# An encoder layer on one core: the query, key and value weights in rows of two heads, half of heads 2 and 3 multiplied early

## What is computed

```
mod = silu(c) @ ada_w + ada_b                  # 2048 x 12288: shift1, scale1, gate1, shift2, scale2, gate2
h   = rms_norm(x) * norm1_g * (1 + scale1) + shift1
q, k, v = split(h @ w_in, 3)                   # w_in 2048 x 6144, 8 heads, 256 columns per head and part
for each head: two softmaxes of q k^T * 128^-0.5 - slope * |distance|, a = p0 - lambda * p1, o = a @ v
x1  = x + gate1 * (rms_norm(o) @ w_out)        # w_out 2048 x 2048
router: top group, top 2 of its 8 experts; SwiGLU experts, 32 of 2048 -> 2 x 512 -> 2048
out = rms_norm(x1 + gate2 * experts) * final_g
```

## Time and profile before

| | us |
|---|---|
| median of 3 runs | 1552.8 (1551.68 to 1553.72) |
| the profiled execution, its own time | 1552.36 |
| its span in the trace | 1550.6 |
| busy: PE, DVE, ACT, POOL | 1166.8, 630.0, 185.2, 118.0 |
| TensorE's mean granted clock | 0.883 of full speed |
| moved by DMA | 577.87 MB, mean 373 GB/s |

### The profile page before, as it was taken

One profiled execution on the slowest core, in us unless ns is written; L12 is line 12 of the kernel. 1 busy time (PEld: TensorE's weight loads), 2 busy tenths in 40 slices (PEclk: granted clock), 3 DMA queues, 4 the chain that ended last, 5 costly groups with the idle time before them and its releaser, 6 DMA issues.

```text
span 1550.6 us, 21165 instructions
## 1 busy us (share of the span) xinstructions
PE 1166.8 (75%) x8538; PEld 760.2 (49%) x8538; DVE 630.0 (41%) x1128; ACT 185.2 (12%) x391; POOL 118.0 (8%) x146
## 2 busy tenths in 40 slices
PE   2298899999999998876657657657657657756655
PEld 2187688888888887433324224224213223323322
DVE  6576775755886112354214213213213213213214
ACT  3000322222224211130000000000000000000002
POOL 4232111101211000000000000000000000000001
PEclk9599899999999999997978878888888878878978
DMA  9997999989998754799999999999999999999996
GB/s 312 348 349 267 340 371 368 356 299 354 319 373 289 278 198 176 303 429 373 429 427 427 430 427 428 430 427 428 430 427 428 430 427 429 428 427 430 425 427 242
DMA packets 128520, 577.87 MB, mean 373 GB/s; under 512 B 10474, under 2 KB 76096, under 8 KB 102996
## 3 DMA queue, kind: packets, MB, share of 16 engines
q1 hardware_dynamic: 101572, 474.37, 76.1%
q0 software_dynamic: 26896, 102.77, 18.4%
HBM read 575.02 MB, written 2.10 MB: 372 GB/s over the span
## 4 chain that ended last, share of the span: by engine, by line
PE 51%; DMA 37%; DVE 7%; another core or an unknown queue 2%; issue 1%; ACT 1%; SPq 0%; DVEq 0%; ACTq 0%
DMA ring<-in_moe_w_gu_dram 19%; DMA ring<-in_moe_w_d_dram 13%; PE psum L589 11%; PE psum L897 7%; PE psum L680 5%; PE psum L599 5%; PE psum L808 5%; PE psum L926 5%; DMA ring<-in_da_w_in_dram 4%; PE psum L949 3%; DVE arena L1216 2%; PE psum L630 2%; PE psum L672 2%; PE psum L570 1%
## 5 line engine op out<-in xcount | busy, mean ns | idle before, releaser
L897 PE MATMUL psum<-ring,ada_ring 128*32 128x256 f32 x3712 | 274.8, 446 | 141.2 <-DMA ring<-in_moe_w_gu_dram 141.2
L1216 DVE SCALAR_TENSOR_TENSOR arena<-ada_ring,silu_c,arena 128x512 f32<-128x512 f32 x360 | 270.6, 752 | 26.8 <-DMA ada_ring<-in_ada_w_dram 15.3
L897 PEld LDWEIGHTS psum<-ring,ada_ring 128*32 128x32 f32 x3712 | 124.0, 121 | 288.5 <-DMA ring<-in_moe_w_gu_dram 188.6
L926 PE MATMUL psum<-ring,arena 128*32 128x512 f32 x960 | 155.4, 792 | 30.3 <-ACT arena L1136 16.2
L589 PE MATMUL psum<-region_b,ring 128*128 128x256 f32 x768 | 169.5, 382 | 0.0
L589 PEld LDWEIGHTS psum<-region_b,ring 128*128 128x128 f32 x768 | 146.5, 192 | 19.4
L1559 DVE TENSOR_TENSOR arena<-psum,arena 32x512 f32<-32x512 f32 x108 | 74.2, 687 | 188.1 <-PE psum L926 176.6
L1542 DVE TENSOR_SCALAR arena<-arena 128x128 f32<-128x128 f32 x32 | 7.3, 227 | 347.9 <-ACT arena L1130 347.9
L456 POOL DMA_DIRECT2D ada_ring<-in_ada_w_dram x128 | 97.5, 764 | 371.1 <-DVE arena L1216 363.7
L1130 ACT ACTIVATE arena<-psum 128x128 f32<-128x128 f32 x32 | 8.9, 277 | 782.5 <-PE psum L897 737.9
L926 PEld LDWEIGHTS psum<-ring,arena 128*32 128x32 f32 x960 | 35.9, 132 | 126.0 <-issue 81.8
(11 more groups left out here) (229 smaller groups left out, 893.6 us busy)
## 6 DMA issues: line engine op xcount, KB each, us to landing
ring<-in_moe_w_gu_dram SPq DMA_DIRECT2D x124, 2048.0 KB, 25.6
ring<-in_moe_w_d_dram SPq DMA_DIRECT2D x62, 2048.0 KB, 24.7
ada_ring<-in_ada_w_dram POOLq DMA_DIRECT2D x64, 1024.0 KB, 9.9
ring<-in_da_w_in_dram SPq DMA_DIRECT2D x24, 2048.0 KB, 27.7
ada_ring<-in_ada_w_dram POOLq DMA_DIRECT2D x64, 512.0 KB, 9.7
ring<-in_da_w_out_dram SPq DMA_DIRECT2D x8, 2048.0 KB, 25.8
ring<-in_moe_w_d_dram SPq DMA_DIRECT2D x8, 512.0 KB, 18.7
region_a<-in_x_dram SPq DMA_DIRECT2D x1, 2048.0 KB, 13.6
```

The lines of the kernel that those rows point to most:

```text
L897: last = mm(psum[32 * n:32 * n + 32, B_GU, 0:256].rearrange("p (a b) -> p a b", a=2), x_items[:, k, SLOTS * i:SLOTS * (i + 1)], w[:, :, n ...
L926: last = mm(psum[32 * n:32 * n + 32, B_D + i % 2, :], hid_t[:, k, :], w[:, kk, n, :], start=k == 0, stop=k == FT - 1)
L1216: ins = v.scalar_tensor_tensor(out=acc[:, par, :], in0=w, scalar=silu_c[:, k:k + 1], in1=acc[:, par, :], op0=ALU.mult, op1=ALU.add)
```

## The change

1. **Rows of two heads.** W_in is loaded for two heads at a time, 512 columns (2 KB) per row. Heads 0 and 1, and the first half of heads 2 and 3: by quarters of the features (4 tiles, 1 MiB for each of q, k, v), two quarters of heads 0 and 1 in slots 0 to 2, two of heads 2 and 3 in slots 3 to 5. The second half of heads 2 and 3, and heads 4 to 7: by halves of the features (8 tiles, 2 MiB). A wide slot of heads 4 to 7 is released by the odd head of the pair, two slots with each product.
2. **Blocks of adaLN.** Blocks 0 and 1 stay. Blocks 2 to 7 are now 512 columns of scale1 (even) and of shift1 (odd), in rows of 2 KB, so `h_t` becomes ready in steps of 2, 2, 4, 4 and 4 tiles (`STEPS`).
3. **Half of heads 2 and 3 early.** Twelve pieces `pair_part(q, u)` of 8 matmuls (tiles 4q to 4q + 3) go among the early ones. ACT keeps each in SBUF (`keep_part`, 12 x 128x512), DVE adds the two quarters (3 x 128x1024). Later `rest_product` multiplies tiles 8 to 15 (16 matmuls), and DVE adds the kept half while it copies the product (`keep_rest`).
4. **The chunks.** Beside heads 2 and 3 DVE has 5 chunks each, beside heads 4 to 6 12 each and beside head 7 9, and PE has three sums in each of heads 4 to 7. The loops over heads are written out. `transpose_out(2)` moves into the first product of head 4.

The core of the diff (the semaphore counts follow from it):

```diff
+        STEPS = ((0, 2), (2, 4), (4, 8), (8, 12), (12, 16))
...
-            for n, (h, j) in enumerate(EARLY):
-                sp.wait_ge(ada_used, ADA_CH * EARLY_STEP[n] + 1)
-                sp.dma_start(slot16(n), w_in[:, :, h * VD + D * j:(h + 1) * VD + D * j]).then_inc(w_loaded[n], 16)
-            with sp.Fori(1, HEADS // 2) as pair:
-                load_head(pair * 2, 0)
-                load_head(pair * 2 + 1, 1)
+            sp.wait_ge(ada_used, 2)
+            load_early(0)
+            sp.wait_ge(ada_used, 6)
+            load_pair(0)
+            sp.wait_ge(ada_used, 9)
+            load_early(1)
+            sp.wait_ge(ada_used, 13)
+            load_pair(1)
+            sp.wait_ge(ada_used, 18)
+            sp.wait_ge(w_used, 1)
+            load_early(2)
+            sp.wait_ge(ada_used, 24)
+            sp.wait_ge(w_used, 3)
+            load_early(3)
+            for j in range(3):
+                sp.wait_ge(part_done, 8 + 2 * j)
+                sp.dma_start(wide_slot(3 + j), w_in[:, 8:16, pair_cols(j)]).then_inc(w_loaded[3 + j], 16)
+            load_wide(2)
+            load_wide(3)
...
+            load_ada(0, 0, halves=True)
+            load_ada(1, ADA_BLK // 2, halves=True)
+            for s in range(1, 4):
+                load_ada(2 * s, D + ADA_BLK * s)
+                load_ada(2 * s + 1, ADA_BLK * s)
...
+            def wide_product(h, j, between=None):
+                n = 6 * (h // 2) + 2 * j
+                bank_free(h, j)
+                for a in range(2):
+                    if a and between:
+                        between()
+                    for k in range(KT):
+                        at = n + k // 8
+                        if a == 0 and k % 8 == 0:
+                            pe.wait_ge(w_loaded[at % RING], 16 * whole_loads(at))
+                        last = product(B_Q + j, j, wide_slot(at % RING), k % 8, k, h % 2, a, start=k == 0,
+                                       stop=k == KT - 1)
+                if h % 2:
+                    last.then_inc(w_used, 2)
...
+            pe.wait_ge(h_ready, 2)
+            for n in range(6):
+                if n == 4:
+                    sum_mod(1, 1)
+                early_part(n, 0)
+
+            pe.wait_ge(h_ready, 4)
+            for n in range(6):
+                last = early_part(n, 1)
+                if n == 5:
                     last.then_inc(w_used, 1)
...
+                    sum_mod(2, 0)
+                pair_part(0, n)
+            sum_mod(3, 1)
+            pe.wait_ge(h_ready, 8)
+            for n in range(6):
+                pair_part(1, n)
+                if n == 4:
+                    sum_mod(4, 0)
+                if n == 5:
+                    sum_mod(5, 1)
+                last = early_part(n, 2)
+            last.then_inc(w_used, 2)
+            pe.wait_ge(h_ready, 12)
+            for n in range(6):
+                if n == 3:
+                    sum_mod(6, 0)
+                if n == 5:
+                    sum_mod(7, 1)
+                last = early_part(n, 3)
...
+            rest_product(2, 0)
+            rest_product(2, 1)
+            transpose_probs(1)
+            sum_mod(9, 1)
+            rest_product(2, 2)
+            attend(1, 1)
+            scores(2, 0)
+            rest_product(3, 0)
+            transpose_out(1)
+            rest_product(3, 1)
+            transpose_probs(2)
+            sum_mod(10, 0)
+            rest_product(3, 2)
+            attend(2, 0)
+            scores(3, 1)
+            head(4, 0, 11, between=lambda: transpose_out(2))
```

More of the change, by code:

```diff
@@ L593, in v_product @@
[L593 to L604, removed]
@@ new lines, in early_part @@
+            def early_part(n, s):
+                i, j = EARLY[n]
+                k0, k1 = STEPS[s]
+                q = k0 // 4
+                if k0 % 4 == 0:
+                    pe.wait_ge(early_loaded[3 * (q % 2) + j], 16 * (q // 2 + 1))
+                for a in range(2):
+                    for k in range(k0, k1):
+                        last = product(EARLY_BANK[n], j, half_slot(j, q % 2), k % 4, k, i, a,
+                                       start=k == 0 and a == 0, stop=k == KT - 1, skip_group_check=True)
+                return last
@@ L1055, in _ @@
             copy_out(0)
[L1056 to L1061 removed]
+            exps(1)
+            turn_acc(9, 1)
+            copy_probs(1)
+            norm_out(1)
+            exps(2)
+            copy_out(1)
+            turn_acc(10, 0)
+            copy_probs(2)
+            norm_out(2)
+            head(4, 0, 11, out_late=True)
+            head(5, 1, 14)
+            head(6, 0, 17)
+            head(7, 1, 20)
             exps(HEADS - 1)
@@ L1282, in out_rstd, with chunks, keep_rest @@
                 v.reciprocal(omid, omid).then_inc(o_rstd, 1)
-            def head(h, b, par, third=False, ahead=2):
+            def chunks(first, n):
+                for at in range(first, first + n):
+                    ada_chunk(at // ADA_CH, at // ADA_CH % 2, at % ADA_CH)
+                    if at % ADA_CH == ADA_CH - 1 and at // ADA_CH > 8:
+                        b = at // ADA_CH - 1
+                        keep_mod(b, b % 2, 4 * b)
+            def keep_rest(h, j):
+                if h == 2:
+                    dve.wait_ge(rest_done, j + 1)
+                else:
+                    dve.wait_ge(w_used, 10 + j)
+                dst = (q_t, k_t, v_tok)[j][:, h % 2, :, :].rearrange("p a b -> p (a b)")
+                v.scalar_tensor_tensor(out=dst, in0=psum[:, B_Q + j, :], scalar=HD ** -0.5 if j == 0 else 1.0,
+                                       in1=part0(h - 2, j), op0=ALU.mult, op1=ALU.add).then_inc(rest_ready, 1)
@@ L1309, in _, with head @@
-            ada_chunk(8, 0, 0)
-            ada_chunk(8, 0, 1)
+                keep_rest(h, 0)
+                chunks(first, 2)
+                keep_rest(h, 1)
+                chunks(first + 2, 3)
+                keep_rest(h, 2)
+                out_rstd(h - 1)
+            def head(h, first, ahead=4):
+                add_bias(h - 1)
+                combine(h - 1)
+                chunks(first, 8)
+                out_rstd(h - 1)
+                chunks(first + 8, ahead)
+            chunks(32, 4)
```

285 lines of the change are left out of this document (165 added, 120 removed).

## The result

The changed kernel takes **1558.46 us** (median of 5 runs, 1555.5 to 1560.77), the kernel before 1552.3 beside it: ratio 1.0039, 95% interval 1.0022 to 1.0056. It is slower by about 6 us, where 1543.0 was forecast, and lies just outside the range of 1527 to 1557. The profiled execution took 1555.5 us, its span is 1553.8.

A forecast was written before the change was run, and what follows sets the result against it. PE was taken to bound heads and output product, DMA the experts, a circle of waits the early stage. 17 - 43.4 + 2 + 15 = -9.4 on 1552.36 gave 1543.0 us, range 1527 to 1557.

The forecast's parts named there:

- Prices: Unit costs for PE, DVE, ACT and DMA, including 388 GB/s with 2 KB rows and 35% for SP's queue.
- Term 1: Early stage, up to head 2's first product: later start, 207 us instead of 189.98, +17 us.
- The bound of +25: Early stage's upper bound: SP's queue stays at 21%, first quarter 16 us later, of which some 7 remain.
- Term 2: Heads 2 and 3: half products shorten them from 97.0 to 53.6 us, -43 us; copies and additions cost nothing.
- term 3: Heads 4 and 5: one more sum each and the moved transposes, +2 us.
- Term 4: Head 6: loads late because only head 5 frees the pair's slots, 12 us idle, +15 us with cold start.
- Term 5: Behind head 7: output product's loads still in time, 0 us, bound 0 to +3.
- The slower outcome: Rival: SP's queue keeps its 21% share, delaying early stage and head 6; +5 us, 1557, chance 0.15.
- the wash: Rival: terms of loss each some 5 us larger (two cold stretches, DVE's additions in the chain); 1552, chance 0.09.
- DVE's waits for sums 2 and 4: Sign in the early stage: DVE idle 15 us or more twice, for these sums.
- the gap in the key product of head 6: Sign: PE idle 8 to 14 us there, W_in as releaser; no gap or over 20 us would mean wrong.
- sum 7 later than 176: Sign of being wrong in the early stage: this sum was expected near 169 us, between 162 and 176.

The follow-up runs named there:

- e2: Changed kernel with heads 4 to 7 loaded one head at a time (1 KB rows, a slot freed by every product), early stage untouched; 1539.5 us.
- e10: Changed kernel with only the PE list edits of e1 and e5, loads of heads 4 to 7 still in rows of two heads; 1544.18 us.
- e9: e5 with ACT making tiles ahead of copies and half products 4 and 5 woven between the fourth block's first parts; 1516.66 us.
- e1: Changed kernel with sums 1 to 7 placed earlier in PE's list, all else the same; 1550.6 us.
- e3: Changed kernel with the edits of e1 and e2 together; 1531.28 us.
- e5: e3 with the parts of heads 0 and 1 ahead of the half products of heads 2 and 3 in PE's third block; 1523.12 us.
- e8: Changed kernel loading one of four feature tiles per early quarter of heads 2 and 3, with one matmul a piece instead of four; 1534.89 us once.
- e4: Changed kernel with one matmul of four in each early piece of heads 2 and 3, loads and copies unchanged; 1535.14 us once.

## Why the prediction was wrong

**Prices, right.** The first quarter's share was forecast at 35% of the bytes from equal turns of packets; from 38 to 50 us it was 792 packets against 791, 1.56 of 4.59 MB, 34%. The Trainium skill (DMA: Bandwidth & Descriptors, Queues, rings and completion order) has the engines go round the queues packet by packet; the trace agrees, here and with the 1 KB rows of e2. 2 KB rows were taken at 388 GB/s; where the link was full the windows give 376 to 388. It was not full throughout: from 260 to 400 us 385 to 390 was forecast, and the mean is 344: from 323 to 337 us SP's queue moved no packet.

**Term 1, the failed step: +17 forecast, +28.7 measured.** The chain was the right one, with its first links too short. The first quarter counted at 50.1 and not 46: SP issued it at 20.87, and its first packets moved after 24. The two parts and the sum behind it took 7.2 us (granted clock 0.55) where 5 were counted, although the forecast names the half clock and two parts at it come to 6.9 by its own prices. So sum 1 ended at 57.3 and not 51. From there the links held: sum 2 ended at 89.3 (83), eight tiles at 103.6 (97), sum 4 at 137.3 (131), each 6.3 to 6.6 later than forecast. Because the sums stand behind a fixed number of parts, nothing in the chain takes up an early delay. Then sum 7 ended at 178.6 (169), 3.2 more: 41.3 us for the 11 chunks, their sums and waits, where 38 was counted; DVE stood 1.4 and 0.9 us for sums 5 and 6, and sum 7 took 1.87 us and not 0.79. Behind it came 1.8 (56 matmuls at a granted clock of 0.83 at their start) and 0.3 more. The bound of +25 stood for a share of 21%, which did not come; it had no place for a late start or a colder clock, and was passed all the same. Its own working is off too: 3.15 MB at 77 GB/s would come 18 us later than at 136, not 16, and that only 7 of them would remain is given without a reason. That the first 6.3 us are handed on whole is read from the trace; no run took the late start out of the change by itself.

**What the runs add to term 1.** The loss is not a price of the early half products as such. e10 keeps all their work and bytes, and head 2 starts at 203.5 instead of 218.7; e9 comes to 195.5, 5.5 behind the kernel before, with 42.7 us taken out of heads 2 and 3.

**Term 2 and term 3, right** within 0.9 and 0.1 us; the copies and additions counted at nothing cost nothing.

**Term 4, the mechanism right, the size 4.5 us low.** The first gap is 9.34 where 12 was forecast. The later ones are 5.92 where "1 to 2 us late" stood, for the reason that the chunk queue would run dry and SP's would get the whole rate: the chunk queue moved 8.81 MB in the 40 us, 220 GB/s, and SP's 6.37 MB, 159 GB/s, more than the 136 of an even turn but far from 388. And there are two cold stretches, 2.2 and 1.8 us (12.60 and 12.13 against 10.36), where one was counted.

**Term 5, right.** From the output product's start to the span's end it is 1069 to 1074 us in before, the change and e1, e2, e3, e5, e9 and e10, whose starts differ by 41 us. The profiled execution of the change, the fastest of its five, has 1068.9 of this, 2.9 less than before; that is within this spread, and so its whole span is only 3.2 us longer where the medians differ by 6.2.

**The rivals.** The slower outcome came, at its price (+5 forecast, +6 measured), but not by its mechanism: the share stayed at 34%, far from the 21% on which it rested. Nearest to what happened is the wash, "terms of loss each some 5 us larger", which had 0.09: term 4 was larger by 4.5, with two cold stretches as it says, but term 1 by 12, and the time is 6 us above its 1552. That the time is close to the slower rival's 1557 is chance. Of the marks named ahead, DVE's waits for sums 2 and 4 (15.85 and 21.02) and the gap in the key product of head 6 (9.34) came as said; sum 7 later than 176, a sign of being wrong, came too (176.85), head 4 started at 271.3 and not 261, and the output product 16 us late.

**Open.** e8's head 2 starts 2.8 us sooner than e4's and its output product 1.0 us sooner (462.93 against 463.90); 1.7 us go to the first product of head 2, which takes 15.75 us there and 14.06 in e4. One execution each can't show a gain of 1 us. How an earlier release by half pairs, in 2 KB rows, would do in head 6 was not tried.

## What to carry to other kernels

Where one engine's list holds both bulk work and the short steps that release another engine, count how long each short step stands behind bulk work, and check whether the link idles meanwhile: here 243 GB/s of 386 pointed to the order and not the bytes, and e10 bore it out. Order bulk work by when its data is issued. Wider rows gave rate (387 GB/s against 372 in e2, from 360 to 380 us), but with them slots came free later; in e2, with half the row length and a slot freed by each product, the output product came 19.6 us sooner.

## What was not expected of the hardware

- SP issued the first quarter at 20.87, and from 21 to 26 us q1 moved 0.17 MB beside 1.58 on q0; from 26 to 31 it was 0.65 beside 1.16. From 19 to 24 us q1 moved no packet, with the link full of chunks. So this load began some 4 us after its issue; the forecast had no such term.
- An issue of SP can itself stand for long, and everything behind it in SP's list with it: 13.53 us for one in the chain above, 22 us for the three of the second early quarter in e10 (issued at 49.35) where the same three took 1.47 in the change (issued at 61.02). What such an issue waits for no run shows.
- Where both queues had work all the time, packets were shared evenly at both row lengths: 792 to 791 at 2 KB (38 to 50 us) and, less the small ones, some 6056 to 5887 at 1 KB (e2, 340 to 420 us), against chunks of 3.8 to 3.9 KB packets. From 380 to 420 us in the change SP's queue got more than that, 42% of the bytes.
